# One modulation half vector moved from TensorE to GpSimd inside the attention stage of a diffusion backbone

## The chip, the cores and the metric

The kernel runs on one core of one Trainium2 chip. The metric is device time in microseconds: the median of the runs. All arithmetic is on float32 data.

## The reference, cut to what matters

Two layers over 256 latent tokens of width 2048, with 256 context tokens. Every layer first makes six modulation vectors from a conditioning vector, and then uses them to shift, scale and gate its sub-layers:

```
silu_c = silu(c)                                        # (1, 2048)
sh_m, sc_m, gt_m, sh_f, sc_f, gt_f = split(silu_c @ w_mod[l] + b_mod[l], 6)
ux = rmsnorm(x, g[0]) * (1 + sc_m) + sh_m
f, q, k, v = split(ux @ w_in)                           # layer 0
mix = concat(fourier_mix(f), window_attention(q, k, v, k_ctx, v_ctx, sink)) @ w_out
x = x + gt_m * rmsnorm(mix, g[1])
x = x + gt_f * rmsnorm(relu(modulate(x, sh_f, sc_f) @ w1)**2 @ w2, g[3])
```

`w_mod[l]` is 2048 x 12288 of float32, 100 MB a layer, of which a half vector is 1024 columns: sixteen slabs of 128 rows by 1024 columns, 512 KB each. A half vector is the sum over the 2048 rows of `silu(c)[row] * w_mod[row, 1024 columns]`.

## The kernel before, in words

Each weight slab (512 KB, half of it or all of it per step) comes by a transfer that SyncE issues into one of four slots `raw`, ScalarE rounds it into `whi` (`hi`, L894), VectorE subtracts to get the remainder `wlo` (`lo`, L1279), and TensorE multiplies both parts.

The half vectors of the modulation (`UNITS`, L48, numbered 0 to 19 after the first four) are computed beside the large products, in one of two ways. Most are summed by VectorE: a slab of `w_mod` lands in `mraw` (two slots; a few in `kv`), and one SCALAR_TENSOR_TENSOR adds slab times `cs[:, k]`, the column of silu(c) that belongs to the slab's 128 rows, onto an accumulator of 128 x 1024 (L1310). The sum over the 128 partitions is taken at the end, by matmuls with ones or by GpSimd. Two of them, units 2 and 3 (`MIX_UNITS`), are summed by TensorE alone: `mix_slab` (L671) multiplies a slab in `early` (four slots are used) by a 128 x 32 operand whose first columns are silu(c), in banks 6 and 7 of PSUM, accumulating over 16 slabs, and ScalarE copies each finished row out (`copy_mix_row`, L1088).

The change lies in the stage that computes the Fourier part. TensorE (L762) walks t = 0 to 23. Step t does, in this order: one slab of the Fourier projection (`fourier_slab`, twelve matmuls, L664 to L666) or, from t = 16, a piece of the discrete Fourier transforms (L727, L741); the turning of one tile of attention probabilities (`turn_probs`, L704); the scores of one head and half (`scores`, L694); on odd t from 7 the values of one head (`values`, L713); and for t = 2 to 17 two slabs of `mix_slab` (L682). VectorE's step t takes the row maximum of the scores that TensorE made in step t - 1 (`row_max`, L1552), makes `wlo` of slab W_F + 3 + t, then the softmax denominator, then one slab of the units 0, 1 and 4 (L1310). ScalarE's step t makes `whi`, the exponentials, copies and normalizes the probabilities, and at t = 10 and t = 18 (`MIX_COPIES`) it first copies a mix row out of PSUM.

SyncE issues everything in one order (L404 to L411). For each slab number w it issues: the weight slab w, once `wlo` of slab w - 4 is made; one slab into `mraw`, once VectorE has used the slab that lay there; then, from w = W_F + 6 on, the pair of mix slabs given by `MIX_LOADS`. The first pair waits, besides, until the product before the stage is done. Pair n, used in TensorE's step n + 2, is issued at w = W_F + 7 + n for n of 2 and more. GpSimd does nothing before the end of the stage.

At t = 22 TensorE turns the finished row of unit 2 into columns (`unit_columns`), picking a few partitions with `sel`; unit 3's row is used in the next stage as a gate.

Of the kernel before, what the change touches and what calls it, by code (L numbers as in the profile page):

```python
# [7 lines left out]
ALU = mybir.AluOpType  # L8
# [4 lines left out]
P = 128  # L13
# [4 lines left out]
SLOTS = 4  # L18
# [8 lines left out]
HALF = D // 2  # L27
UNIT = KC
# [11 lines left out]
W_KV, W_F = 2 * SL, 3 * SL  # L40


def slab_of(pg):
# [4 lines left out]
UNITS = [(0, 4, 0), (0, 4, 1), (0, 3, 0), (0, 2, 0), (0, 2, 1), (0, 3, 1), (0, 5, 0),  # L48
         (1, 0, 0), (1, 0, 1), (1, 1, 0), (1, 1, 1), (1, 2, 0), (0, 5, 1), (1, 2, 1),
         (1, 4, 0), (1, 4, 1), (1, 3, 0), (1, 3, 1), (1, 5, 0), (1, 5, 1)]  # L50
MIX_UNITS = (2, 3)
FIRST_UNITS = (0, 1, 4)
FIRST_ACC = (1, 0, 1)
ACT_PAIRS = (1, 3, 5)
# [53 lines left out]
def backbone_program(nc, x_in, c_in, ctx_in, c_ctx, w_mod, b_mod, gains, att_w_in, sink, att_w_out,  # L108
                     conv_w_in, conv_w, conv_w_out, mlp_w1, mlp_w2, tables, out):
    with ExitStack() as ctx:  # L110
# [3 lines left out]
        def sem(name):  # L114
            return ctx.enter_context(nc.semaphore(name))
# [14 lines left out]
        red = sb("red", [P, HALF])  # L130
# [9 lines left out]
        cs = sb("cs", [P, 2 * KC])  # L140
# [6 lines left out]
        ps = ctx.enter_context(nc.psum_tensor("ps", [P, 8, 512], F32))  # L147
# [18 lines left out]
        prob = [yf[:, 512 * i:512 * i + 512] for i in range(2)]  # L166
        probT = [ff[:, 2048 + 1024 * i:3072 + 1024 * i].rearrange("p (k q) -> p k q", k=4) for i in range(2)]
        row = (red[:, :], acc[:, 1, :])
        mix_row = (red[:, :], ff[:, 0:HALF])
        first_row = diag[:, 2, :]  # L170

        yt = yf.rearrange("p (a d) -> p a d", a=2)
# [22 lines left out]
        start_landed = [sem(f"start_landed{i}") for i in range(START_SLOTS)]  # L195
        m_landed = [sem(f"m_landed{i}") for i in range(2)]
        kvm_landed = [sem(f"kvm_landed{i}") for i in range(2)]
        mix_landed = [sem(f"mix_landed{i}") for i in range(SLOTS)]
        mix_used, mix_copied, first_row_ready, columns_done, gate_spread, gate_step = (sem(n) for n in (
            "mix_used", "mix_copied", "first_row_ready", "columns_done", "gate_spread", "gate_step"))  # L200
        hi_ready, lo_ready, slab_used, m_used = (sem(n) for n in ("hi_ready", "lo_ready", "slab_used", "m_used"))
# [76 lines left out]
        def _(sp):  # L278
# [98 lines left out]

            def mix_pair(n):

                for i in (2 * n, 2 * n + 1):  # L380
                    if i >= SLOTS:
                        sp.wait_ge(mix_used, i - (SLOTS - 1))
                    un, k = MIX_UNITS[i // UNIT], i % UNIT
                    sp.dma_start(early[:, i % SLOTS, :], w_mod[0, k * P:(k + 1) * P, mcol(un):mcol(un) + HALF]
                                 ).then_inc(mix_landed[i % SLOTS], 16)

            def first_unit_slab(m):

# [13 lines left out]
            for w in range(SL, slab_of(PG_WO) + SL):  # L402
                att_slab(w)
                for m in FIRST_LOADS.get(w, ()):  # L404
                    first_unit_slab(m)
                if w == W_F + 6:
                    sp.wait_ge(slab_used, W_KV + SL)
                for n in MIX_LOADS.get(w - (W_F + 7), ()):
                    mix_pair(n)
            for m in LAST_LOADS:  # L410
                first_unit_slab(m)  # L411
            sp.wait_ge(o_ready, HEADS)
# [47 lines left out]
        def _(pe):  # L460
# [209 lines left out]

            def mix_slab(n):  # L671

                i, k = divmod(n, UNIT)
                if k == 0:
                    if i:
                        pe.wait_ge(mix_copied, i)
                    else:
                        pe.wait_ge(mod_ready, 1)
                pe.wait_ge(mix_landed[n % SLOTS], 16 * (n // SLOTS + 1))
                for half in range(2):  # L680
                    tile = 32 * ((k + 2 * half) % 4)
                    last = pe.matmul(ps[tile:tile + 32, 6 + half, :], crs[:, k, :],  # L682
                                     early[:, n % SLOTS, half * 512:(half + 1) * 512], start=(k < 4),
                                     stop=(k >= KC - 4), tile_position=(0, tile))
                last.then_inc(mix_used, 1)

# [58 lines left out]
            def unit_columns(un, bank, src, pick):  # L745

                for c in range(KC // 2):
                    last = pe.matmul(ps[:, bank, 16 * un + 2 * c:16 * un + 2 * c + 2], src[:, c * P:(c + 1) * P],
                                     pick, start=True, stop=True)
                last.then_inc(columns_done, 1)  # L750
# [9 lines left out]
            for t in range(24):  # L760
                if t < 2 * SL:
                    fourier_slab(t)  # L762
                else:
                    stage_dft, g = DFT_ORDER[t - 2 * SL]
                    (channel_dft if stage_dft else token_dft)(g)
                if 0 <= t - 4 < 2 * HEADS:
                    turn_probs(t - 4)
                if 0 <= t - 2 < 2 * HEADS:
                    scores(t - 2)
                if t >= 7 and t % 2 and t // 2 - 3 < HEADS:  # L770
                    values(t // 2 - 3)
                for n in mix_slabs(t):
                    mix_slab(n)
                if t == 21:
                    pe.wait_ge(pt_copied, 2 * HEADS)
                    pe.wait_ge(m_used, 2 * UNIT)
                    unit_columns(1, 2, acc[:, FIRST_ACC[1], :], ones[:, 0:2])
                if t == 22:
                    pe.wait_ge(mix_copied, 2)
                    unit_columns(2, 2, mix_row[0], sel)  # L780
                if t == 23:
                    pe.wait_ge(m_used, len(FIRST_UNITS) * UNIT)
                    spread_gate(ones, acc[:, FIRST_ACC[2], :], 6)
# [10 lines left out]
            def out_waits(s):  # L794

                if s == 0:
                    pe.wait_ge(o_ready, HEADS)
                if s == 1:
                    pe.wait_ge(first_row_ready, 1)
                    pe.wait_ge(mod_ready, 3)  # L800
                    spread_gate(first_row, mix_row[1], 2)
                if s >= SL // 2:
                    pe.wait_ge(f_ready, s - SL // 2 + 1)

# [88 lines left out]
        def _(act):  # L893
# [173 lines left out]
            def fourier_high(g):  # L1067
                act.wait_ge(fb_done, g + 1)
                if g:
                    act.wait_ge(y_summed, 2 * g)  # L1070
                act.activation(odd, two_tiles(g % 2)[:, :, 0:P - 1], ACT.Copy).then_inc(odd_copied, 1)
                if g == 0:
                    act.wait_ge(rope_done, 5)
                if g == 1:
                    act.wait_ge(mix_used, UNIT * len(MIX_UNITS))
                if g >= 2:
                    act.wait_ge(f_ready, g - 1)
                act.activation(y_sum[g % 2][:, :, 0:P + 1:P], two_tiles(g % 2)[:, :, P - 1:T:P],
                               ACT.Copy).then_inc(edges_copied, 1)
                act.wait_ge(edges_copied, g + 1)  # L1080
                act.wait_ge(y_summed, 2 * g + 2)
                act.activation(u[:, 2 * g:2 * g + 2, 0:T], y_sum[g % 2], ACT.Copy).then_inc(fb_hi, 1)
# [2 lines left out]
                act.wait_ge(pv_done, hd + 1)  # L1085
                act.activation(h[:, 8 + hd, 0:T], ps[:, 3, (hd % 2) * T:(hd % 2 + 1) * T], ACT.Copy).then_inc(o_hi, 1)

            def copy_mix_row(i):  # L1088
                act.wait_ge(mix_used, UNIT * (i + 1))
                act.activation(mix_row[i].rearrange("p (m n) -> p m n", m=2), ps[:, 6:8, :],  # L1090
                               ACT.Copy).then_inc(mix_copied, 1)

            for t in range(25):
                if t in MIX_COPIES:
                    copy_mix_row(MIX_COPIES.index(t))
                if t <= 16:
                    hi(W_F + 3 + t, (3 + t) % SLOTS)
                if 0 <= t - 3 < 2 * HEADS:
                    probabilities(t - 3)
                if 0 <= t - 5 < 2 * HEADS:  # L1100
                    probs_turned(t - 5)
                if t >= 8 and t % 2 == 0 and t // 2 - 4 < HEADS:
                    o_high(t // 2 - 4)
                if 0 <= t - 3 < 2 * HEADS:
                    normalized(t - 3)
                if 0 <= t - 2 * SL < 2 * FG:
                    stage_dft, g = DFT_ORDER[t - 2 * SL]
                    (fourier_high if stage_dft else token_transformed)(g)
# [169 lines left out]
        def _(dve):  # L1278
# [297 lines left out]
            def fourier_sums(g):  # L1576

                even = two_tiles(g % 2)[:, :, P:T - 1]
                dve.wait_ge(odd_copied, g + 1)
                dve.wait_ge(edges_copied, g + 1)  # L1580
                if g == 1:
                    dve.wait_ge(mix_used, UNIT * len(MIX_UNITS))
                if g >= 2:
                    dve.wait_ge(f_ready, g - 1)
                dve.tensor_tensor(y_sum[g % 2][:, :, 1:P], even, odd, ALU.subtract).then_inc(y_summed, 1)
                dve.tensor_tensor(y_sum[g % 2][:, :, T - 1:P:-1], even, odd, ALU.add).then_inc(y_summed, 1)
# [343 lines left out]

        @block.gpsimd
        def _(pool):
            pool.wait_ge(gate_spread, 1)
            pool.memset(acc[:, 1, :], 0.0).then_inc(acc_zeroed, 1)
            pool.wait_ge(columns_done, 3)
# [17 lines left out]

OUT_ORDER = tuple((s + SL // 2) % SL for s in range(SL))
DFT_ORDER = ((0, 0), (0, 1), (1, 0), (0, 2), (1, 1), (0, 3), (1, 2), (1, 3))
MIX_COPIES = (10, 18)
MIX_LOADS = {t: (t if t > 0 else t + 1,) for t in range(-1, 16) if t != 1}
UNITS_BESIDE = ((2,), (0, 1, 0, 1, 0, 0, 0, 1), (1, 1, 1, 1, 2, 2, 2, 2), (2, 3, 3),
                (1, 1, 1, 1, 1, 1, 1, 1, 1, 1, 1, 1, 1, 1, 1, 1, 1), (1, 1, 1, 1, 1, 1))
UNIT_COUNTS = tuple(n for part in UNITS_BESIDE for n in part)  # L1960
# [49 lines left out]

def mix_slabs(t):

    return range(2 * (t - 2), 2 * (t - 1)) if 2 <= t < 18 else ()


LOAD_CTX, LOAD_X = 3, 5
# [63 lines left out]
```

## Time and profile before

| | us |
|---|---|
| median of 3 runs (2239.07 to 2245.07) | 2241.67 |
| the profiled execution, its own time | 2239.6 |
| its span | 2237.8 |
| TensorE busy in the span | 2182.6 |
| VectorE busy | 1655.1 |
| ScalarE busy | 1018.5 |
| GpSimd busy, 32 instructions | 98.8 |
| the 16 DMA engines, mean rate over the span | 265 GB/s |

The profile is of one execution. Its span is cut into engines' busy time, a chain of waits (what released what, followed back from the end), groups of instructions, and transfers. The stage of the change runs from about 201 us (first mix slabs issued) to about 327 us. Matmul durations include the pipeline, so successive starts tell the rate and not the duration. A line of a helper, as L899 or L1282, collects all its uses.

### The profile page before, as it was taken

The page shows a single profiled execution, that of the slowest core. Times are in us where ns is not written, and L with a number is a line of the kernel's source. Part 1 is how long each engine was busy: PE and PEld are TensorE (multiplying, and loading weights), DVE is VectorE, ACT ScalarE, POOL GpSimd, SP SyncE. Part 2 cuts the span into 40 slices and gives each one's busy share as a digit, 9 for nine tenths or more (in the row PEclk, how much of TensorE's full clock was granted, in tenths as well). Part 3 has the DMA queues.
Part 4 walks back from the last instruction along what each step waited for, and adds up shares of the span by engine and source line. Part 5 has one row for each costly group of instructions (what it writes and reads, how often), then busy time and mean ns, then how long its engine had stood idle before and what let it go on. Part 6 is the DMA issues. An engine that isn't in the chain of part 4 may idle for free.

```text
span 2237.8 us, 30998 instructions
## 1 busy us (share of the span) xinstructions
PE 2182.6 (98%) x11355; PEld 1802.6 (81%) x11355; DVE 1655.1 (74%) x1792; ACT 1018.5 (46%) x1269; POOL 98.8 (4%) x32
## 2 busy tenths in 40 slices
PE   7899999999999999999989999999999999999998
PEld 3388578788888888888868888878888888888887
DVE  1288658888798788788988988989887554655655
ACT  3183545644344344344454444456534444443443
POOL 0000000001011011010101101100011000000000
PEclk8899999999999999999999999999999999999999
DMA  9988968688887977888867888887887666656664
GB/s 374 387 285 304 373 208 300 228 293 286 284 289 263 316 266 273 312 292 296 286 218 276 271 301 286 280 299 234 283 289 247 190 194 190 188 192 194 202 197 150
DMA packets 253891, 592.59 MB, mean 265 GB/s; under 512 B 18082, under 2 KB 18610, under 8 KB 253234
## 3 DMA queue, kind: packets, MB, share of 16 engines
q1 hardware_dynamic: 253746, 590.63, 77.8%
q8 instruction: 95, 1.56, 0.3%
q14 instruction: 50, 0.41, 0.0%
HBM read 588.46 MB, written 2.10 MB: 264 GB/s over the span
## 4 chain that ended last, share of the span: by engine, by line
PE 87%; DMA 4%; DVE 4%; ACT 2%; issue 2%; SPq 0%; DVEq 0%; ACTq 0%
PE ps L512 30%; PE ps L518 15%; PE ps L587 11%; PE ps L588 11%; PE ps L589 11%; DMA early<-in_w_mod_dram 1%; PE ps L551 1%; DMA raw<-in_mlp_w_dram 1%; ACT whi L899 1%; DVE wlo L1282 1%; DVE acc L1292 1%; PE ps L475 1%; DMA x<-in_x_dram 1%; PE ps L682 1%; PE ps L713 1%
## 5 line engine op out<-in xcount | busy, mean ns | idle before, releaser
L1282 DVE TENSOR_TENSOR wlo<-raw,whi 128x1024 fp32r<-128x1024 f32 x712 | 899.5, 1267 | 435.8 <-ACT whi L899 434.4
L899 ACT ACTIVATE whi<-raw 128x1024 fp32r<-128x1024 f32 x712 | 751.3, 1059 | 949.0 <-PE ps L589 371.7
L512 PE MATMUL ps<-u,whi 128*128 128x512 f32 x2944 | 928.0, 397 | 5.9 <-DVE u L1445 2.4
L518 PEld LDWEIGHTS ps<-u,wlo 128*128 128x128 f32 x2944 | 553.6, 188 | 131.0
L518 PE MATMUL ps<-u,wlo 128*128 128x256 f32 x2944 | 579.0, 278 | 0.0
L587 PE MATMUL ps<-whi,h 128*128 128x512 f32 x1216 | 475.9, 391 | 6.5 <-DVE wlo L1282 6.3
L589 PE MATMUL ps<-whi,h 128*128 128x512 f32 x1216 | 474.1, 390 | 0.0
L588 PE MATMUL ps<-wlo,h 128*128 128x512 f32 x1216 | 474.1, 390 | 0.0
L512 PEld LDWEIGHTS ps<-u,whi 128*128 128x128 f32 x2944 | 449.2, 189 | 13.2 <-issue 10.5
L1292 DVE SCALAR_TENSOR_TENSOR acc<-mraw,cs,acc 128x1024 f32<-128x1024 f32 x240 | 306.7, 1278 | 3.9 <-DMA mraw<-in_w_mod_dram 3.7
L587 PEld LDWEIGHTS ps<-whi,h 128*128 128x128 f32 x1216 | 228.7, 188 | 57.8 <-DVE wlo L1282 10.3
L589 PEld LDWEIGHTS ps<-whi,h 128*128 128x128 f32 x1216 | 228.7, 188 | 48.0
L588 PEld LDWEIGHTS ps<-wlo,h 128*128 128x128 f32 x1216 | 228.8, 188 | 47.1 <-issue 0.5
L1947 POOL PARTITION_ALL_REDUCE red<-acc x13 | 84.3, 6487 | 1134.2 <-DVE acc L1292 432.3
L999 ACT ACTIVATE tmp<-ps 128x512 f32<-128x512 f32 x92 | 53.6, 595 | 34.9 <-PE ps L518 34.7
L1222 ACT ACTIVATE h<-fq 128x512 fp32r<-128x512 f32 x64 | 39.5, 634 | 29.9 <-DVE fq L1790 29.9
L551 PE MATMUL ps<-early,junk 128*32 128x512 f32 x192 | 40.7, 731 | 12.5 <-DMA early<-in_w_mod_dram 12.5
L1783 DVE TENSOR_TENSOR fq<-ps,tmp 128x512 f32<-128x512 f32 x64 | 43.0, 685 | 10.6 <-ACT tmp L999 10.6
L1310 DVE SCALAR_TENSOR_TENSOR acc<-mraw,cs,acc 128x1024 f32<-128x1024 f32 x35 | 44.9, 1282 | 6.0 <-DMA mraw<-in_w_mod_dram 5.4
L1801 DVE TENSOR_TENSOR h<-fq,h 128x512 fp32r<-128x512 f32 x64 | 41.1, 682 | 0.0
L1790 DVE SCALAR_TENSOR_TENSOR fq<-fq 128x512 f32<-128x512 f32 x64 | 41.0, 681 | 0.0
L551 PEld LDWEIGHTS ps<-early,junk 128*32 128x32 f32 x192 | 6.6, 121 | 29.2 <-DMA early<-in_w_mod_dram 14.4
(203 smaller groups left out, 1239.1 us busy)
## 6 DMA issues: line engine op xcount, KB each, us to landing
raw<-in_mlp_w_dram SPq DMA_DIRECT2D x512, 512.0 KB, 4.7
mraw<-in_w_mod_dram SPq DMA_DIRECT2D x278, 512.0 KB, 5.5
raw<-in_conv_w_in_dram SPq DMA_DIRECT2D x96, 512.0 KB, 5.2
early<-in_w_mod_dram SPq DMA_DIRECT2D x80, 512.0 KB, 8.1
raw<-in_att_w_in_dram SPq DMA_DIRECT2D x40, 512.0 KB, 5.8
raw<-in_att_w_out_dram SPq DMA_DIRECT2D x32, 512.0 KB, 6.0
raw<-in_conv_w_out_dram SPq DMA_DIRECT2D x32, 512.0 KB, 6.2
raw<-in_w_mod_dram SPq DMA_DIRECT2D x16, 512.0 KB, 8.0
```

The source lines that it names most:

```text
L512: return pe.matmul(ps[:, 4 * slot + m, :], whi[:, s % SLOTS, cols], src[:, k, :], start=(k == 0), stop=False)
L518: return pe.matmul(ps[:, 4 * slot + m, 0:T], wlo[:, s % SLOTS, cols], src[:, k, 0:T], start=False, stop=(k == KC - 1))
L551: last = pe.matmul(ps[tile:tile + 32, (0, 2, 0, 6)[hv] + n, :], crs[:, k, :], start_slab(w)[:, n * 512:(n + 1) * 512], start=(k < 4), stop ...
L587: pe.matmul(o, high, whi[:, s % SLOTS, cols], start=first, stop=False)
L588: pe.matmul(o, high, wlo[:, s % SLOTS, cols], start=False, stop=False)
L589: last = pe.matmul(o, low, whi[:, s % SLOTS, cols], start=False, stop=final)
L899: act.activation(whi[:, s, :], raw[:, s, :], ACT.Copy).then_inc(hi_ready, 1)
L999: act.activation(tmp[half][:, :, :], right(slot, half), ACT.Copy).then_inc(b_copied, 1)
L1282: dve.tensor_tensor(wlo[:, s, :], raw[:, s, :], whi[:, s, :], ALU.subtract).then_inc(lo_ready, 1)
L1292: dve.scalar_tensor_tensor(out=a, in0=src, scalar=cs[:, bass.ds(k, 1)], in1=a, op0=ALU.mult, op1=ALU.add).then_inc(m_used, 1)
L1310: dve.scalar_tensor_tensor(out=a, in0=src, scalar=cs[:, k:k + 1], in1=a, op0=ALU.mult, op1=ALU.add).then_inc(m_used, 1)
L1947: pool.partition_all_reduce(red[:, :], acc[:, un % 2, :], P, RADD).then_inc(unit_summed, 1)
```

## The change

Unit 3 stays on TensorE, unit 2 goes to GpSimd, slab by slab: the slab is multiplied in its slot by `cs[:, k]` and then added to `red`. The four slots of `early` are divided: two for TensorE's slabs, which come as a pair every second step once both of the pair before are used, and two for GpSimd's, one in every step. `PAIR` is 2, `UNIT` is 16. Lines that only follow from a new name are left out.

```diff
-MIX_UNITS = (2, 3)
+MIX_UNIT, POOL_UNIT, PAIR = 3, 2, 2
@@ SyncE
             def mix_pair(n):
-                for i in (2 * n, 2 * n + 1):
-                    if i >= SLOTS:
-                        sp.wait_ge(mix_used, i - (SLOTS - 1))
-                    un, k = MIX_UNITS[i // UNIT], i % UNIT
-                    sp.dma_start(early[:, i % SLOTS, :], w_mod[0, k * P:(k + 1) * P, mcol(un):mcol(un) + HALF]
-                                 ).then_inc(mix_landed[i % SLOTS], 16)
+                if n:
+                    sp.wait_ge(mix_used, PAIR * n)
+                for k in (PAIR * n, PAIR * n + 1):
+                    sp.dma_start(early[:, k % PAIR, :], w_mod[0, k * P:(k + 1) * P, mcol(MIX_UNIT):mcol(MIX_UNIT) + HALF]
+                                 ).then_inc(mix_landed[k % PAIR], 16)
+            def pool_row(k):
+                if k >= PAIR:
+                    sp.wait_ge(row_used, k - PAIR + 1)
+                sp.dma_start(early[:, PAIR + k % PAIR, :],
+                             w_mod[0, k * P:(k + 1) * P, mcol(POOL_UNIT):mcol(POOL_UNIT) + HALF]
+                             ).then_inc(row_landed[k % PAIR], 16)
...
                 for n in MIX_LOADS.get(w - (W_F + 7), ()):
                     mix_pair(n)
+                if 0 <= w - (W_F + 6) < UNIT:
+                    pool_row(w - (W_F + 6))
@@ TensorE, t == 22
-                    pe.wait_ge(mix_copied, 2)
-                    unit_columns(2, 2, mix_row[0], sel)
+                    pe.wait_ge(row_used, UNIT)
+                    pe.wait_ge(mix_copied, 1)
+                    unit_columns(2, 2, red, ones[:, 0:2])
@@ ScalarE
-            def copy_mix_row(i):
-                act.wait_ge(mix_used, UNIT * (i + 1))
+            def copy_mix_row():
+                act.wait_ge(mix_used, UNIT)
...
-                if t in MIX_COPIES:
-                    copy_mix_row(MIX_COPIES.index(t))
+                if t == MIX_COPY:
+                    copy_mix_row()
@@ GpSimd, ahead of all its other work
+            pool.wait_ge(silu_step, 3)
+            pool.wait_ge(row_t, 4)
+            for k in range(UNIT):
+                pool.wait_ge(row_landed[k % PAIR], 16 * (k // PAIR + 1))
+                if k == 0:
+                    pool.tensor_scalar(red[:, :], early[:, PAIR + k % PAIR, :], cs[:, k:k + 1], None,
+                                       ALU.mult).then_inc(row_used, 1)
+                else:
+                    slab = early[:, PAIR + k % PAIR, :]
+                    pool.tensor_scalar(slab, slab, cs[:, k:k + 1], None, ALU.mult).then_inc(row_scaled, 1)
+                    pool.wait_ge(row_scaled, k)
+                    pool.wait_ge(row_used, k)
+                    pool.tensor_tensor(red[:, :], red[:, :], slab, ALU.add).then_inc(row_used, 1)
@@ tables
-MIX_COPIES = (10, 18)
-MIX_LOADS = {t: (t if t > 0 else t + 1,) for t in range(-1, 16) if t != 1}
+MIX_COPY = 18
+MIX_LOADS = {2 * n - 1 + (n > 0) * 2: (n,) for n in range(8)}
 def mix_slabs(t):
-    return range(2 * (t - 2), 2 * (t - 1)) if 2 <= t < 18 else ()
+    return (t - 2, t - 1) if 2 <= t < 18 and t % 2 == 0 else ()
```

## Rows read from the trace of the kernel before

**Rows 1.** The page, busy time, share of the span and instructions of the engines.
```profile
PE 2182.6 (98%) x11355; PEld 1802.6 (81%) x11355; DVE 1655.1 (74%) x1792; ACT 1018.5 (46%) x1269; POOL 98.8 (4%) x32
```

**Rows 2.** Stretches: engines' busy us (instructions), granted clock, DMA share, GB/s.
```profile
226.00:262.00 36.00, 35.39 (x172) 21.75 (x176) 24.02 (x46) 20.69 (x40) 0.00 (x0) 1.00 1.03 397
262.00:304.70 42.70, 42.68 (x215) 26.35 (x208) 28.63 (x56) 22.45 (x48) 0.00 (x0) 1.00 0.93 329
```

**Rows 3.** Chain of waits in time, the stage: start us, us, what.
```profile
217.14 8.82 DMA early<-in_w_mod_dram
226.01 1.05 PE ps L682 x4
...
255.81 1.07 PE ps L682 x8
...
261.84 1.00 PE ps L682 x8
...
268.83 1.00 PE ps L682 x8
...
274.07 1.00 PE ps L682 x8
...
281.04 0.99 PE ps L682 x8
...
297.47 1.00 PE ps L682 x8
...
303.63 1.07 PE ps L682 x8
...
305.64 0.29 ACT sm L1041
...
310.57 0.63 PE ps L704 x4
```

**Rows 4.** SyncE's queue in time: start us, us, line, transfer.
```profile
222.40 1.21 SPq L384 DMA_DIRECT2D early<-in_w_mod_dram  x2
...
278.01 0.33 SPq L395 DMA_DIRECT2D mraw<-in_w_mod_dram  x1
```

**Rows 5.** Transfer groups, 262 to 300 us, then 210 to 230: count, size, median us to landing.
```profile
early<-in_w_mod_dram SPq DMA_DIRECT2D x12, 512.0 KB, 5.7
mraw<-in_w_mod_dram SPq DMA_DIRECT2D x6, 512.0 KB, 6.8
...
early<-in_w_mod_dram SPq DMA_DIRECT2D x8, 512.0 KB, 8.0
```

**Rows 6.** VectorE in time: parts of one step, and the last row maximum.
```profile
274.11 0.30 DVE L1557 TENSOR_TENSOR ps<-ps,tab 128x128 f32<-128x128 f32 x1 [2.76 <-PE ps L694]
...
275.30 1.22 DVE L1282 TENSOR_TENSOR wlo<-raw,whi 128x1024 fp32r<-128x1024 f32 x1
...
276.70 1.28 DVE L1310 SCALAR_TENSOR_TENSOR acc<-mraw,cs,acc 128x1024 f32<-128x1024 f32 x1
...
303.00 0.21 DVE L1561 TENSOR_SCALAR sm<-sm,nsink 128x1 f32<-128x1 f32 x1
```

**Rows 7.** GpSimd's groups: busy us, mean ns, idle before and its releasers.
```profile
L1947 POOL PARTITION_ALL_REDUCE red<-acc x13 | 84.3, 6487 | 1134.2 <-DVE acc L1292 432.3 <-DVE t L1357 325.6 <-DVE tab L1378 247.3
L1950 POOL MEMSET acc<- 128x1024 f32 x11 | 10.5, 957 | 0.7
```

**Rows 8.** GpSimd, then VectorE in time, beside one of the all-reduces.
```profile
619.38 7.06 POOL L1947 PARTITION_ALL_REDUCE red<-acc  x1 [82.91 <-DVE tab L1378]
...
620.38 5.56 DVE L1282 TENSOR_TENSOR wlo<-raw,whi 128x1024 fp32r<-128x1024 f32 x1
625.86 1.27 DVE L1292 SCALAR_TENSOR_TENSOR acc<-mraw,cs,acc 128x1024 f32<-128x1024 f32 x1
```

**Rows 9.** ScalarE in time: its copies of the mix rows.
```profile
256.90 1.03 ACT L1090 ACTIVATE red<-ps 128x1024 f32<-128x1024 f32 x1 [4.53 <-PE ps L682]
...
304.72 1.02 ACT L1090 ACTIVATE fq<-ps 128x1024 f32<-128x1024 f32 x1 [3.19 <-PE ps L682]
```

More of the change, by code:

```diff
@@ L168, in backbone_program @@
         row = (red[:, :], acc[:, 1, :])
-        mix_row = (red[:, :], ff[:, 0:HALF])
+        mix_row = ff[:, 0:HALF]
         first_row = diag[:, 2, :]
@@ L197, in backbone_program @@
         kvm_landed = [sem(f"kvm_landed{i}") for i in range(2)]
-        mix_landed = [sem(f"mix_landed{i}") for i in range(SLOTS)]
+        mix_landed = [sem(f"mix_landed{i}") for i in range(PAIR)]
+        row_landed = [sem(f"row_landed{i}") for i in range(PAIR)]
+        row_used, row_scaled = sem("row_used"), sem("row_scaled")
         mix_used, mix_copied, first_row_ready, columns_done, gate_spread, gate_step = (sem(n) for n in (
@@ L671, in mix_slab @@
             def mix_slab(n):
-                i, k = divmod(n, UNIT)
+                k = n
                 if k == 0:
[L675 to L679, printed above, removed]
+                    pe.wait_ge(mod_ready, 1)
+                pe.wait_ge(mix_landed[k % PAIR], 16 * (k // PAIR + 1))
                 for half in range(2):
@@ L682, in mix_slab @@
                     last = pe.matmul(ps[tile:tile + 32, 6 + half, :], crs[:, k, :],
-                                     early[:, n % SLOTS, half * 512:(half + 1) * 512], start=(k < 4),
+                                     early[:, n % PAIR, half * 512:(half + 1) * 512], start=(k < 4),
                                      stop=(k >= KC - 4), tile_position=(0, tile))
@@ L800, in out_waits @@
                     pe.wait_ge(mod_ready, 3)
-                    spread_gate(first_row, mix_row[1], 2)
+                    spread_gate(first_row, mix_row, 2)
                 if s >= SL // 2:
@@ L1074, in fourier_high @@
                 if g == 1:
-                    act.wait_ge(mix_used, UNIT * len(MIX_UNITS))
+                    act.wait_ge(mix_used, UNIT)
                 if g >= 2:
@@ L1086, in o_high @@
                 act.activation(h[:, 8 + hd, 0:T], ps[:, 3, (hd % 2) * T:(hd % 2 + 1) * T], ACT.Copy).then_inc(o_hi, 1)
-            def copy_mix_row(i):
-                act.wait_ge(mix_used, UNIT * (i + 1))
-                act.activation(mix_row[i].rearrange("p (m n) -> p m n", m=2), ps[:, 6:8, :],
+            def copy_mix_row():
+                act.wait_ge(mix_used, UNIT)
+                act.activation(mix_row.rearrange("p (m n) -> p m n", m=2), ps[:, 6:8, :],
                                ACT.Copy).then_inc(mix_copied, 1)
             for t in range(25):
-                if t in MIX_COPIES:
-                    copy_mix_row(MIX_COPIES.index(t))
+                if t == MIX_COPY:
+                    copy_mix_row()
                 if t <= 16:
@@ L1581, in fourier_sums @@
                 if g == 1:
-                    dve.wait_ge(mix_used, UNIT * len(MIX_UNITS))
+                    dve.wait_ge(mix_used, UNIT)
                 if g >= 2:
```

## The prediction

> **What bounds the kernel now.** I read the page first. TensorE is busy for 98% of the span and GpSimd for 4% [rows 1], so work that leaves TensorE can count, and GpSimd has room. But a share over the whole says nothing of one stage, so I then cut the stage by windows and followed the chain of waits through it. From 226 us to 304.7 us TensorE has almost no gap, and at the same time the DMA engines stand at a share of 1.03 and 0.93, with 397 and 329 GB/s [rows 2]. Two limits lie close together. The chain [rows 3] shows which one ends last: it runs through TensorE from 226.0 us to 304.7 us. One step of TensorE without the values takes 274.07 - 268.83 = 5.24 us and one with them 281.04 - 274.07 = 6.97 us, in each 1.0 us of it the two mix slabs; so two steps take 12.2 us. At three places the chain leaves TensorE: at 217.14 us a mix transfer of 8.82 us is waited for; the step from 255.81 to 261.84 us takes 6.03 us, 0.8 more than 5.24; and after the last mix slabs, which end at 304.7 us, TensorE goes on only at 310.57 us.
>
> The last two are ScalarE's. Its queue stands at the mix copy until TensorE has finished the row (4.53 and 3.19 us idle [rows 9]), with `whi` and the exponentials queued behind.
>
> **Part 1: TensorE's mix slabs, 16 of 32 removed.** They leave the odd steps. From the end of step 4 to the end of step 16's mix, that is from 227.06 to 298.47 us [rows 3], six odd steps each lose 1.0 us, and the copy at t = 10 goes with its 0.8 us: 6.0 + 0.8 = -6.8 us, all of it on the chain.
>
> **Part 2: the copy at t = 18.** The row is now finished in step 16, so ScalarE copies while it would be idle. What is late next is the row maximum of the last scores, ready at 303.00 + 0.21 = 303.2 us [rows 6], against the exponential's start at 305.64 us [rows 3]: -2.4 us.
>
> **Part 3: the first pairs.** Before, step 4 used the pair issued ahead of 217.14 us. Now it uses pair 1, issued at w = W_F + 10, where the queue stood at 222.40 us [rows 4]; its place follows an `mraw` slab for which VectorE's use of an earlier one is awaited, and that does not change. Its second slab goes out at about 223.0 us, and by the 8.0 us of this stretch [rows 5] it lands at 231.0 us against 225.97: with its 1.05 us of matmuls, +4.9 us. Bounds: landing in 5.7 us [rows 5] and an issue 1 us earlier +1.6; 8.82 us [rows 3] and an issue 1 us later, behind a row wait, +6.8.
>
> **Part 4: later pairs.** Their cover gets thinner. The pair for step t used to be issued one step earlier relative to its use, with four slots. Now its issue follows VectorE's step t - 1: the scores of step t - 2 end at 274.07, VectorE's slab of the unit at 276.70 + 1.28 = 277.98 us [rows 6], `mraw` is issued at 278.01 us [rows 4] and the pair is out at about 278.8 us, 4.7 us after the scores. Between the scores of t - 2 and of t TensorE has 12.2 - 1.0 = 11.2 us plus what it waited at the mix of t - 2. With a landing time L and a delay b of VectorE, the wait is 4.7 + b + L - 11.2, less the wait of the pair before; so it comes about at every second pair. Rows give L as 5.7 to 8.0 us [rows 5]; the demand rises from four slabs (2.1 MB) in 6.1 us to the same in 5.6 us, 375 GB/s, close to the 397 of [rows 2], so I take 7.0. For b I take 1.0 (part 5). Then the wait is 1.5 us at three of the pairs: +4.5 us. Bounds: with b = 0 and L = 5.7 nothing; with b = 3.0 and L = 8.0, 4.5 us three times, +13.5.
>
> **Part 5: GpSimd's rows.** The trace has no elementwise instruction of two operands on GpSimd. Nearest are a MEMSET of the same 128 x 1024, 0.957 us, which only writes, and the PARTITION_ALL_REDUCE, 6.49 us [rows 7]. Two instructions a row give between 1.9 and 13.0 us. I take 0.96 for the multiplication, twice that for the addition of two operands, since both are streams like the MEMSET, and 0.3 us for the two waits: 3.2 us, and 1 us for waiting behind VectorE, 4.2 us in all. It is not on the chain by itself. But SyncE stands at each `pool_row` until row k - 2 is used, and behind it in the queue are the weight slab, the `mraw` slab and the pair of the next step. With two slots a row costs (L + 4.2) / 2 = 5.6 us a step, just what TensorE's 5.6 us hides; I put +1 us for this edge. Row 15 is issued in about TensorE's step 15 and done 11 us later, ahead of step 22, which needs it.
>
> VectorE feels it too. During an all-reduce, a `wlo` subtraction took 5.56 us and ended as the all-reduce did, 0.5 us apart, where one takes 1.22 with GpSimd idle [rows 6]; the 1.27 us accumulation followed [rows 8]. So an instruction of VectorE with two operands in SBUF seems to wait for GpSimd's. VectorE has two such large ones in each step, at 1.2 and 1.28 us; GpSimd's two hold about 2.9 of 5.6 us, so either is met half the time and then costs about half of 1 to 2 us: b = 1.0 us a step, up to 3.0 if each is met in full. TensorE reads `wlo` slabs made three steps ahead, so b counts only through part 4.
>
> The Trainium skill, SBUF - State Buffer, section "Who interferes with whom", says the same as a rule: a VectorE instruction with two SBUF inputs and a GpSimd instruction that reads SBUF exclude one another for the whole instruction. The row above agrees for the all-reduce. By that rule a MEMSET would hold nothing, and both new instructions would. The skill's GPSIMD Engine Reference, "Performance versus the Vector engine", has 4497 ns for an addition of 2048 float32, by which 1024 would be an estimated 2.3 us and the row 0.4 us longer; the sum would be the same within 1 us.
>
> **The sum.** Against the profiled execution's 2239.6 us (span 2237.8 and 1.8 around it): -6.8 - 2.4 + 4.9 + 4.5 + 1.0 = +1.2 us, 2240.8. The median of the runs stands 2.1 us above that execution, so 2243 us. After the stage nothing refills: the chain from 310.57 us on is TensorE's, so the shift stays.
>
> **The rivals.**
> (a) The 11.2 us cover everything. Part 4 and the edge are zero and part 3 is at its lower bound: -6.8 - 2.4 + 1.6 = -7.6, 2234 us. For it: a late `mraw` and pair landed in 5.7 and 6.8 us [rows 5]. Against: the rate must rise towards the highest that the stage reached. Chance 0.2.
> (b) VectorE is held by GpSimd at both its large instructions in every step. b = 3.0 and L = 8.0: part 4 at +13.5, part 3 at +6.8: -6.8 - 2.4 + 6.8 + 13.5 + 1.0 = +12.1, 2254 us. For it: [rows 8]; against: most of VectorE's 5.6 us has no such pair of operands active. The Trainium skill's rule named above is this one. Chance 0.17.
> (c) GpSimd is the pacer, and this ends on the slower side: the wait of `pool_row` holds the whole queue. From L + row above 11.2 us it decides; it costs more than the old 6.0 us a step from a row of 5.5 us at L = 6.5. With 8 us a row, (6.5 + 8) / 2 = 7.25 us a step, 12 steps at +1.3 us over the 71.4 us before: +15.6 in place of parts 1 and 4; with -2.4 + 4.9 it is +18, 2260 us. For it: the only computing row of GpSimd is 6.49 us; against: that one crosses partitions, the MEMSET does not. Chance 0.13.
> (d) The transfers alone are the floor, so that TensorE's work was hidden anyway. The stretch moves at 329 GB/s in its second half against 397 in its first [rows 2], so it isn't at its floor; this bounds (a) and has no case of its own.
>
> **How the numbers follow.** The forecast holds 0.5, with 2237 to 2249 as its own range. 0.3%, about what a measurement of this kernel tells from no change, is 6.7 us: 2235 to 2248.4. Half and more of (a) is faster, with a trace of the forecast: 0.15. (b), (c) and the upper edge of the forecast are slower: 0.3. The rest is 0.55. The range of 8 in 10 is 2234 to 2258.
>
> **What would show it.** Right: step 4's mix ends near 232 us; pairs of steps of 11.2 to 12.7 us after; TensorE's gap after step 17 shorter by 2.4 us; VectorE's `wlo` and unit instructions beside GpSimd longer than 1.3 us in part; the sum of GpSimd's two instructions near 3 us. Wrong: SyncE's waits at `pool_row` above 1 us a step, with TensorE waiting for `wlo` (c); pair waits at each even step above 3 us (b); the stage shorter by over 7 us (a). The whole is wrong if the time changes outside 201 to 327 us.

## The result and the profile after

The changed kernel takes 2251.45 us, median of 6 runs (2249.72 to 2252.33), against 2241.57 us of the kernel before, also 6 runs: the ratio is 1.004 with a 95% interval of 1.003 to 1.0051, so it is slower by 0.4%, 9.9 us between the medians. The profiled execution took 2251.9 us (span 2250.1), 12.3 us more than the one of before.

The engines' busy time, first line of the page, answers to [rows 1]:

```profile
PE 2176.7 (97%) x11291; PEld 1800.6 (80%) x11291; DVE 1680.0 (75%) x1792; ACT 1017.6 (45%) x1268; POOL 190.9 (8%) x63
```

TensorE lost 64 matmuls and 5.9 us of busy time. GpSimd gained 92 us for 31 instructions. VectorE still executes 1792 instructions and is busy for 25 us more: the same instructions took longer.

The same stretches as in [rows 2] (engines' busy us in the order TensorE, its weight loads, VectorE, ScalarE, GpSimd, then granted clock, DMA share, GB/s):

```profile
226.00:262.00 36.00, 30.98 (x125) 18.32 (x126) 29.25 (x37) 15.87 (x31) 35.50 (x13) 0.88 0.92 343
262.00:304.70 42.70, 39.28 (x171) 25.86 (x170) 38.02 (x55) 21.82 (x46) 40.16 (x15) 1.00 0.94 337
```

TensorE, which had almost no gap, is now idle for 5.0 and 3.4 us of the two stretches. GpSimd has almost no gap, and VectorE rose from 28.63 to 38.02 us of 42.7 us. The chain of waits through the stage, which answers to [rows 3] (L690 is now the mix matmul, L1291 the `wlo` subtraction, L1319 the accumulation of a unit's slab, L763 the matmuls that spread a gate after the stage):

```profile
216.46 2.85 POOL early L1951
...
219.39 3.09 POOL red L1954
222.50 0.33 SPq L392
...
223.86 6.14 DMA early<-in_w_mod_dram
...
230.04 3.20 PE ps L690 x8
...
263.32 3.03 DVE wlo L1291
...
266.53 1.88 DVE acc L1319
...
275.52 8.01 DMA early<-in_w_mod_dram
...
300.58 9.32 DMA early<-in_w_mod_dram
...
309.94 1.92 PE ps L690 x4
...
321.88 0.63 PE ps L712 x4
...
341.09 1.72 PE ps L763 x4
```

From 226 us on it used to run through TensorE almost alone. Now it goes GpSimd, SyncE's queue, a transfer, and TensorE at step 4; VectorE's long instructions from 238 to 275 us; then transfers of pairs that TensorE waits for at steps 12 and 16. Step 16's mix begins at 309.94 us, where it began at 297.47 [rows 3]. The last gate's matmuls start at 341.09 us; before, they started at 329.79 us:

```profile
329.79 1.72 PE ps L755 x4
```

So 11.3 us of the difference of 12.3 are there by the end of this stage, although it began about a microsecond earlier (the first pair was issued at 200.17 us against 201.34).

What GpSimd's instructions cost, the answer to [rows 7] (groups of the stage; busy us, mean ns, idle before):

```profile
L1951 POOL TENSOR_SCALAR early<-early,cs 128x1024 f32<-128x1024 f32 x15 | 53.5, 3564 | 8.0 <-DMA early<-in_w_mod_dram 8.0
L1954 POOL TENSOR_TENSOR red<-red,early 128x1024 f32<-128x1024 f32 x15 | 36.2, 2414 | 1.2
```

The addition takes 2.41 us where 1.92 was forecast, the multiplication 3.56 us where 0.96 was. A row takes 6.25 us, and from 216.4 us to its last row GpSimd is idle for 3 us in all. VectorE's two large instructions, over 205 to 305 us, first in the changed kernel and then in the kernel before:

```profile
L1291 DVE TENSOR_TENSOR wlo<-raw,whi 128x1024 fp32r<-128x1024 f32 x17 | 35.6, 2092 | 1.1 <-ACT whi L908 1.1
L1319 DVE SCALAR_TENSOR_TENSOR acc<-mraw,cs,acc 128x1024 f32<-128x1024 f32 x16 | 28.6, 1785 | 1.9 <-DMA mraw<-in_w_mod_dram 1.9
```
```profile
L1282 DVE TENSOR_TENSOR wlo<-raw,whi 128x1024 fp32r<-128x1024 f32 x17 | 20.7, 1217 | 4.6 <-ACT whi L899 4.6
L1310 DVE SCALAR_TENSOR_TENSOR acc<-mraw,cs,acc 128x1024 f32<-128x1024 f32 x17 | 21.8, 1283 | 3.6 <-DMA mraw<-in_w_mod_dram 3.6
```

One period shows how they are tied. First GpSimd, then VectorE, in time:

```profile
244.09 2.38 POOL L1954 TENSOR_TENSOR red<-red,early 128x1024 f32<-128x1024 f32 x1
246.44 3.82 POOL L1951 TENSOR_SCALAR early<-early,cs 128x1024 f32<-128x1024 f32 x1
250.35 2.39 POOL L1954 TENSOR_TENSOR red<-red,early 128x1024 f32<-128x1024 f32 x1
252.70 3.82 POOL L1951 TENSOR_SCALAR early<-early,cs 128x1024 f32<-128x1024 f32 x1
```
```profile
244.46 3.09 DVE L1291 TENSOR_TENSOR wlo<-raw,whi 128x1024 fp32r<-128x1024 f32 x1
...
251.37 2.44 DVE L1291 TENSOR_TENSOR wlo<-raw,whi 128x1024 fp32r<-128x1024 f32 x1
...
254.00 1.88 DVE L1319 SCALAR_TENSOR_TENSOR acc<-mraw,cs,acc 128x1024 f32<-128x1024 f32 x1
```

The subtraction begins at 244.46 us, GpSimd's addition ends at 246.47, the subtraction at 247.55: 1.08 us after, about the length of its own work. The second pair of them repeats it (252.74, then 253.81). GpSimd's multiplication, at 246.44 us, began while the subtraction was still at work and took 3.82 us; where no subtraction was at work at its start it took 2.85. The accumulation at 254.00 us starts and ends inside a multiplication and takes 1.88 instead of 1.28 us, so it is slowed and not shut out. A subtraction that begins inside a multiplication is not even slowed:

```profile
216.46 2.84 POOL L1951 TENSOR_SCALAR early<-early,cs 128x1024 f32<-128x1024 f32 x1 [6.06 <-DMA early<-in_w_mod_dram]
217.49 1.21 DVE L1291 TENSOR_TENSOR wlo<-raw,whi 128x1024 fp32r<-128x1024 f32 x1
```

### The profile page after: what moved, and what is told of

The parts are those of the page before. It is cut to its first block, busy times and chain, and to the rows that moved or that the text cites. A ratio compares the mean times of both kernels' runs of the same rounds, so it can differ in the third digit from the quotient of the medians.

```text
span 2250.1 us, 30918 instructions
## 1 busy us (share of the span) xinstructions
PE 2176.7 (97%) x11291; PEld 1800.6 (80%) x11291; DVE 1680.0 (75%) x1792; ACT 1017.6 (45%) x1268; POOL 190.9 (8%) x63
## 4 chain that ended last, share of the span: by engine, by line
PE 78%; DVE 9%; DMA 6%; issue 3%; ACT 2%; SPq 1%; POOL 0%; DVEq 0%; ACTq 0%; POOLq 0%
PE ps L523 30%; PE ps L529 15%; PE ps L598 10%; PE ps L599 10%; PE ps L600 10%; DVE wlo L1291 3%; DMA early<-in_w_mod_dram 2%; PE ps L562 2%; DVE acc L1301 1%; DVE acc L1319 1%; ACT whi L908 1%; DMA raw<-in_att_w_out_dram 1%; DMA raw<-in_mlp_w_dram 1%; DMA raw<-in_conv_w_out_dram 1%; PE ps L486 1%
## 5 line engine op out<-in xcount | busy, mean ns | idle before, releaser
L1291 DVE TENSOR_TENSOR wlo<-raw,whi 128x1024 fp32r<-128x1024 f32 x712 | 916.9, 1292 | 429.9 <-ACT whi L908 428.2
L1301 DVE SCALAR_TENSOR_TENSOR acc<-mraw,cs,acc 128x1024 f32<-128x1024 f32 x240 | 311.2, 1297 | 4.3 <-DMA mraw<-in_w_mod_dram 4.3
L1319 DVE SCALAR_TENSOR_TENSOR acc<-mraw,cs,acc 128x1024 f32<-128x1024 f32 x35 | 52.9, 1513 | 5.0 <-DMA mraw<-in_w_mod_dram 4.5
L1951 POOL TENSOR_SCALAR early<-early,cs 128x1024 f32<-128x1024 f32 x15 | 53.5, 3564 | 8.0 <-DMA early<-in_w_mod_dram 8.0
```

The source lines that it names most:

```text
L1291: dve.tensor_tensor(wlo[:, s, :], raw[:, s, :], whi[:, s, :], ALU.subtract).then_inc(lo_ready, 1)
L1301: dve.scalar_tensor_tensor(out=a, in0=src, scalar=cs[:, bass.ds(k, 1)], in1=a, op0=ALU.mult, op1=ALU.add).then_inc(m_used, 1)
L1319: dve.scalar_tensor_tensor(out=a, in0=src, scalar=cs[:, k:k + 1], in1=a, op0=ALU.mult, op1=ALU.add).then_inc(m_used, 1)
```

## The experiments

Each ratio is to the kernel before, run beside it. In the changed kernel two things could eat the gain: GpSimd's arithmetic, by its row time or by holding VectorE, and the thinner cover of TensorE's pairs.

**GpSimd hardly touches the rows.**

```diff
-                if k == 0: (multiplication into red) else: (multiplication, addition)
+                pool.tensor_scalar(red[:, k:k + 1], early[:, PAIR + k % PAIR, 0:1], cs[:, k:k + 1], None,
+                                   ALU.mult).then_inc(row_used, 1)
```

> The changed kernel, but GpSimd touches only one column of each row's slab (128 x 1), so unit 2's sum is left out; all transfers, slots and waits stay. Pacing theory (SyncE stands at the row waits because GpSimd needs 6.25 us a row) and holding theory (GpSimd's addition holds VectorE's two-operand instructions, so that VectorE's step grows from 4.0 to over 6 us) both expect 2238 to 2242 us, the pairs' later issue being all that is left. The pair theory (the loss is the thinner cover of TensorE's pairs, at step 4 and step 16) expects 2247 to 2252 us.

Measured: 0.9996 (0.9986 to 1.0005), 2242.69 us: 0.7 us above what two of the theories allowed, and far below the third. With the same transfers, slots and waits, the 0.4% is gone. GpSimd's arithmetic is the cause of the loss against before, by one edge or the other, which this run does not separate; but the gain that the shorter steps should bring does not show either. The chain of this run still waits at step 4 and at step 16 for a pair:

```profile
221.27 7.75 DMA early<-in_w_mod_dram
229.07 3.19 PE ps L690 x8
...
292.97 7.79 DMA early<-in_w_mod_dram
300.80 1.05 PE ps L690 x4
```

**Rows free at landing, GpSimd's arithmetic on other data.**

```diff
-                    sp.wait_ge(row_used, k - PAIR + 1)
+                    sp.wait_ge(row_landed[k % PAIR], 16 * (k // PAIR))
@@ GpSimd
+                part = x[:, k // 2 % 2, HALF * (k % 2):HALF * (k % 2 + 1)]
+                if k:
+                    pool.wait_ge(row_used, k)
+                pool.tensor_scalar(red[:, :], part, cs[:, k:k + 1], None, ALU.mult).then_inc(row_scaled, 1)
+                pool.wait_ge(row_scaled, k + 1)
+                pool.tensor_tensor(red[:, :], red[:, :], part, ALU.add).then_inc(row_used, 1)
```

> The changed kernel, but a row's slot is free again as soon as its transfer has landed, and GpSimd does its multiplication and addition, same shapes, on other data that nobody overwrites, so unit 2's sum is left out. GpSimd holds VectorE as before, but its row time no longer reaches SyncE's queue. Pacing theory: 2238 to 2243 us, with wlo subtractions still long. Holding theory: 2247 to 2252 us, VectorE without idle time in the stage.

Measured: 1.0031 (1.0021 to 1.0041), 2249.76 us. SyncE has no wait on GpSimd left, and most of the loss stays. Holding alone can do that: VectorE's `wlo` group has a mean of 1945 ns in this run,

```profile
L1291 DVE TENSOR_TENSOR wlo<-raw,whi 128x1024 fp32r<-128x1024 f32 x17 | 33.1, 1945 | 1.1 <-ACT whi L908 1.1
```

Whether the row waits, 38.9 us of SyncE's time in the changed kernel, add anything of their own stays open: 1.0031 and 1.004 have intervals that overlap. The traces hint that they add something, for the last gate's matmuls start at 335.76 us here and at 341.09 in the changed kernel. The forecast of the holding theory that VectorE would have no idle time failed: it waited 10.0 us for scores between 205 and 305 us.

**Only the addition.**

```diff
-                    pool.tensor_scalar(slab, slab, cs[:, k:k + 1], None, ALU.mult).then_inc(row_scaled, 1)
-                    pool.wait_ge(row_scaled, k)
                     pool.wait_ge(row_used, k)
                     pool.tensor_tensor(red[:, :], red[:, :], slab, ALU.add).then_inc(row_used, 1)
```

> The changed kernel without the multiplications by silu(c) from row 1 on: GpSimd adds each slab as it is, one instruction of 2.4 us a row instead of 6.2 us for two. Pacing theory: SyncE never waits for a row, 2239 to 2243 us. Holding theory: the addition is what holds wlo for its whole length, so a good half of the loss of 10 us stays, 2245 to 2249 us.

Measured: 1.0029 (1.0017 to 1.0042), 2248.29 us. A row costs 2.5 us, GpSimd is idle for 46 us between transfers, and yet two thirds of the loss stay. SyncE still waits 10.9 us for rows, where none was expected, against 38.9. The subtraction is held as before, the accumulation not at all:

```profile
L1291 DVE TENSOR_TENSOR wlo<-raw,whi 128x1024 fp32r<-128x1024 f32 x17 | 32.5, 1909 | 1.1 <-ACT whi L908 1.1
L1319 DVE SCALAR_TENSOR_TENSOR acc<-mraw,cs,acc 128x1024 f32<-128x1024 f32 x17 | 21.8, 1284 | 1.7 <-DMA mraw<-in_w_mod_dram 1.7
```

So the addition holds the subtraction, and in the changed kernel the multiplication is what stretches the accumulation from 1.28 to about 1.8 us. It does not follow that an addition leaves an accumulation alone: in this run none began while an addition was at work, and in the tensor-by-tensor run below one that did was held.

**Pairs one step earlier, nothing else.**

```diff
-MIX_LOADS = {2 * n - 1 + (n > 0) * 2: (n,) for n in range(8)}
+MIX_LOADS = {2 * n - 1 + (n > 0): (n,) for n in range(8)}
```

> The changed kernel with each pair from pair 1 on issued one step earlier in SyncE's queue; nothing else. Pair theory: steps 4 and 16 no longer wait 6 to 8 us for the pair, 2242 to 2246 us. Pacing and holding theories: each step still costs 6.25 us, at most 2 us are won, 2249 to 2252 us.

Measured: 1.001 (1.0 to 1.002), 2245.73 us. The step is worth 0.3%, which the pair theory expected and which is more than the other two allowed. Of the transfers only one wait for `early` of 6 us, ahead of the first row, is left on the chain, and the gate's matmuls start at 333.82 us against 341.09. The profiled execution, 2251.22 us, was the slowest of the ten; at the gate it is 7.3 us ahead of the changed kernel's, at the end 0.7, so it loses the rest after the stage, and its trace counts here for the stage alone.

The chain of this run shows something else. From 209.73 to 299.37 us it lies on GpSimd, whose instructions follow each other without a gap, and SyncE waits 56.2 us for rows:

```profile
218.15 2.86 POOL early L1951
221.08 3.10 POOL red L1954
224.18 3.81 POOL early L1951
```

VectorE is busy for 67.92 of the 70 us from 230 to 300 us, and the multiplications take 3.80 us, with a subtraction at work at their start, so the two pace each other. With the pairs out of the way the row time itself is on the chain. What holding alone costs there was not tested: it would take this order of issue together with rows that are free at landing.

**Both together.** The two edits of the first and the fourth experiment.

> GpSimd touches one column of each slab (unit 2's sum left out), and each pair is issued one step earlier. No row time, no holding, no thin cover: if those three are the whole of what ate the gain, TensorE's shorter odd steps and the copy that no longer waits show here, 6 to 9 us below the kernel before, 2233 to 2236 us. If the transfers are the floor of the stage, it stays at 2239 to 2243 us.

Measured: 0.9966 (0.9954 to 0.9978), 2233.78 us. Here is the gain that the forecast gave to parts 1 and 2. TensorE's chain has no gap from step 6 to the last scores, and two steps take 11.0 us:

```profile
224.59 3.21 PE ps L690 x8
...
248.38 1.00 PE ps L690 x8
...
259.39 1.00 PE ps L690 x8
...
291.40 1.00 PE ps L690 x8
...
321.32 1.72 PE ps L763 x4
```

The last line is the gate's, 8.5 us earlier than in the kernel before. Where the time lies shows in one stretch, from the end of step 4's mix (227.80 us here) to the end of step 16's (292.40):

| | us |
|---|---|
| before | 71.4 |
| this run | 64.6 |
| GpSimd touches one column, pairs as changed | 69.6 |
| the changed kernel | 78.6 |

The four kernels make a table, in per cent against before:

| | pairs as changed | pairs one step earlier |
|---|---|---|
| GpSimd multiplies and adds | +0.40 | +0.10 |
| GpSimd touches one column | -0.04 | -0.34 |

Each number is good to about 0.1, the fourth comes from another session and chip than the second and third, and the first from its own. GpSimd's arithmetic costs 0.44% (9.9 us) with either order of issue, the late issue of the pairs 0.30% (6.7 us) with either use of GpSimd, and what is left when both are gone is -0.34% (7.6 us). That the sums agree to the last digit is chance, and the 0.44% need not have the same way in both columns: on the left the chain is VectorE's and the pairs', on the right GpSimd's.

**The multiplication as a tensor-by-tensor one.**

```diff
-                    pool.tensor_scalar(slab, slab, cs[:, k:k + 1], None, ALU.mult).then_inc(row_scaled, 1)
+                    pool.tensor_tensor(slab, slab, cs[:, k:k + 1].broadcast_to([P, HALF]), ALU.mult).then_inc(row_scaled, 1)
```

> The changed kernel with GpSimd's multiplication written as a tensor-by-tensor one, its second operand the one column repeated 1024 times: computes the same. If it costs like the addition (2.4 us) a row falls from 6.25 to 4.8 us and SyncE no longer waits for rows. Pacing theory: 2243 to 2246 us. Holding theory: now both instructions exclude VectorE's for their whole length, 2248 to 2254 us.

Measured: 1.009 (1.0071 to 1.011), 2261.76 us, above what either theory expected. It is the best case against pacing as the cause of the loss. A row costs less, 2.1 us for the multiplication and 3.1 for the addition, SyncE waits 7.1 us for rows instead of 38.9, and the kernel is slower by another half per cent. VectorE in time shows why; even the softmax denominator, one column by one column, waits for GpSimd:

```profile
255.89 2.30 DVE L1576 TENSOR_TENSOR sm<-sm 128x1 f32<-128x1 f32 x1
...
271.00 0.15 DVE L1576 TENSOR_TENSOR sm<-sm 128x1 f32<-128x1 f32 x1
```

It took 2.30 us in one step and 0.15 us in another, where GpSimd was not at an addition. The group's 13 instructions add up to 18.7 us, and VectorE is busy for 71.8 of 74 us between 226 and 300 us. Here an accumulation, too, meets an addition: it begins 0.05 us after one that runs from 229.48 to 231.84 us, and ends 1.08 us after it:

```profile
229.53 3.39 DVE acc L1319
```

**The copies moved, in the kernel before.** The `if t in MIX_COPIES: copy_mix_row(...)` of ScalarE's step goes from the head of the step to just ahead of its Fourier work.

> The kernel before, with ScalarE's two copies of mix rows placed after the exponentials, probabilities and weight slab of their step instead of ahead of them; TensorE and GpSimd as before. The forecast gave 0.8 us at t = 10 and 2.4 us at t = 18 to these waits: 2238 to 2240 us, 0.15% below. If other waits take their place, no change.

Measured: 0.9988 (0.9979 to 0.9997), 2239.38 us. That is faster than both kernels, by 0.12% over the kernel before. The step from 256.76 to 262.00 us takes the full TensorE period of 5.24 us and no more, where it took 6.03 [rows 3], and the probabilities after step 17 are turned 5.7 us after the mix slabs' start, where it was 6.9:

```profile
256.76 1.00 PE ps L682 x8
...
262.00 1.00 PE ps L682 x8
...
303.77 1.00 PE ps L682 x8
...
309.51 0.63 PE ps L704 x4
```

The copy itself no longer waits; it follows at once on what stands before it in ScalarE's queue:

```profile
258.60 1.03 ACT L1090 ACTIVATE red<-ps 128x1024 f32<-128x1024 f32 x1
```

**Unit 2 left out with its transfers.** The edits of the run with both, and SyncE's `pool_row` call removed; GpSimd's sixteen small instructions read `cs` instead.

> Unit 2 left out wholly, its 16 transfers too; pairs one step earlier. Against the run with rows loaded but hardly touched it tells what 8.4 MB of transfers cost the stage. If transfers press on it: 3 to 6 us lower than that run. If TensorE's chain alone sets it: the same within 1 us.

Measured: 0.9951 (0.9936 to 0.9967), 2231.36 us. Against 0.9966 (0.9954 to 0.9978), 2233.78 us, the intervals overlap and the medians differ by 2.4 us, between the two outcomes that were expected: whether 8.4 MB of transfers less are worth nothing or a few us is not told. The transfers were not the floor at which the kernel before stood, for the run with both edits has them all and is 0.34% faster.

## Why the prediction was right and wrong

The measured time lies in the range of 2234 to 2258 us, and above the 2237 to 2249 that the forecast gave itself. The sign is the forecast one, but +1.2 us was a forecast of next to nothing, so that is luck. The likeliest case, a change within 0.3%, did not come. The terms taken from TensorE's and ScalarE's rows held; those on GpSimd and what it does to VectorE did not. Step by step:

- **Part 1, -6.8 us, and part 2, -2.4 us: shown.** With the two costs taken away, -0.34% is 7.6 us, and the medians of that session differ by 9.1; the two steps of 11.2 us were 11.0, and the stretch from step 4 to step 16 fell from 71.4 to 64.6 us, by 6.8. Part 2 stands in the changed kernel itself: TensorE goes on 6.3 us after the end of the last scores (315.61, then 321.88) and not 8.7 (301.90, then 310.57 [rows 3]), 2.4 us less. The moved copies alone give 0.8 us at t = 10 and 1.2 us at t = 18; the mix slabs of step 17, 1.00 us on the chain there, are most of the rest.
- **Part 3, +4.9 us: right in kind, short in size.** I said that step 4's mix ends near 232 us; it ended at 233.24, from an earlier start, so it cost 7.3 us rather than 4.9 (5.0 by the terms as given: 231.0 + 1.05 - 227.06). The transfer was quicker than forecast, 6.14 us for 8.0, but the pair was issued 1.5 us later, behind the wait until GpSimd had used the second row (L392 at 222.50 us), and the matmuls took 3.20 us, not 1.05, at a lowered clock (below). With little on GpSimd the mix still ended at 232.26 us, at the same clock.
- **Part 4, +4.5 us: the right size without GpSimd, too small with it.** With little on GpSimd, so with b = 0, the stretch was 69.6 us against 64.6: +5.0 us. The equation gives 1.3 us three times with that run's L of 7.8. Parts 3 and 4 together were 0.30% by the ratios, 6.7 us, and 9.3 us by the gate's start in the two traces (330.60 and 321.32), of the 9.4 forecast.
- **Part 5, +1 us and b = 1.0: the step that failed.** The forecast of the stretch from step 4 to step 16 was 71.4 - 6.8 + 4.5 + 1.0 = 70.1 us; it took 78.6. Two things were too small. The first is the price of a row: 0.96 us for the multiplication, after the MEMSET, where it takes 2.85 us undisturbed and 3.56 in the mean. A row is 6.25 us and not 4.2, which keeps GpSimd at work through the whole stage, so that VectorE meets it almost every time: its subtraction grew by 0.88 us and its accumulation by 0.50 us a step. The nearest row was near in shape only: it reads nothing. The bound of 13.0 us for two instructions had held the truth; the value chosen in it was too low. The second, and by the runs the larger, is how far b reaches. I let it count once for a pair, at three pairs. In the changed kernel VectorE itself is the chain from 238.08 to 274.67 us, six steps of 6.1 us without a wait, longer than TensorE's 5.5, so its delays add up from step to step. With the multiplication left out the subtraction grew by 0.69 us, less than the 1.0 that I took, and still 0.29 + 0.04 = 0.33% was lost, 7.4 us. In all, GpSimd's arithmetic cost 0.44%, 9.9 us, the largest term; the +1 us and what b brought to part 4 had been some 4 us.
- **The rivals.** (b), that GpSimd holds VectorE, is what happened: three runs show it, the last of them by making GpSimd's row shorter and the kernel slower. Its condition, b = 3.0 in every step, was too strong; 1.4 us a step was enough, as GpSimd's other edge, the row wait at step 4, came with it. Its 2254 us is nearer to the measured time than the forecast's 2243. (c), the pace of GpSimd, was met by its own number, a row above 5.5 us, and SyncE did wait 38.9 us at `pool_row`; but with the waits gone 0.31% stayed, so in the changed kernel it is a part at most, and that part was not told apart from noise. With the pairs one step earlier the chain is GpSimd's own, and there (c) was neither shown nor ruled out as the cost. (a) failed twice: on GpSimd, and on its cover of 11.2 us, for with GpSimd hardly at work the kernel took 2242.69 us and not 2234, with TensorE waiting for the pair of step 16. (d) was ruled out rightly.
- **The rule of the page.** The Trainium skill, SBUF - State Buffer, "Who interferes with whom", has a two-input VectorE instruction and a reading GpSimd instruction exclude each other for their whole length. For GpSimd's additions this case's traces agree (a subtraction ends 1.08 us after the addition, twice). For its multiplication by a column they agree only in part: one that began beside a subtraction took 1.0 us longer, but of VectorE's instructions with two SBUF inputs an accumulation started and ended inside one, at 1.88 us, and so did a subtraction, at 1.21 us. The measurement decides: VectorE loses 0.6 us or nothing there.

## What to carry to other kernels

Before moving an elementwise sum onto an idle GpSimd, look at what VectorE executes beside it: where VectorE's own instructions read two SBUF operands, each microsecond that GpSimd spends on an addition may be taken from VectorE, idle time in the page's first line or not. A shorter GpSimd instruction is no help if it is one that holds VectorE for longer. And where slots are halved to make room for a second stream, move the remaining loads ahead in the queue by as much as their cover has lost; here that one line was worth 0.3%.

## What was not expected of the hardware

GpSimd multiplies 128 x 1024 float32 by a column in 2.85 us at best, more than the 2.36 us of its addition of two tensors and three times a MEMSET of that shape (0.96 us); by a tensor operand that repeats the column it takes 1.89 us at best. And TensorE's granted clock fell in the changed kernel's stage. TensorE was idle from 216.3 to 219.8 us; the clock was still 1.00 until 220 us and 0.50 from 221 us on. It stayed there through the wait for the pair of step 4, 8.1 us without work up to 230.04 us, and was back at 1.00 from 235 us:

```profile
215.00:220.00 5.00, 1.42 (x7) 0.87 (x6) 4.79 (x8) 1.89 (x5) 3.46 (x2) 1.00 1.04 410
220.00:225.00 5.00, 1.89 (x6) 0.53 (x5) 4.90 (x8) 2.78 (x6) 5.00 (x2) 0.57 0.48 145
225.00:230.00 5.00, 0.00 (x0) 0.00 (x0) 4.90 (x8) 2.03 (x5) 4.92 (x3) 0.50 1.03 409
230.00:235.00 5.00, 4.96 (x14) 1.88 (x15) 1.82 (x2) 0.72 (x1) 4.92 (x3) 0.57 0.91 357
```

At 0.50 of 2.4 GHz, the lower of its two levels, the eight entries of the mix slabs took 3.20 us, where the kernel before spent 1.00 us on such a group. So these waits on TensorE cost about 2 us more than their own length.
